# Writing out the matrix engine's loop over fifteen experts

## The reference, cut to what matters

```python
def ec_moe(h, router_w, w1, w3, w2):
    xt = h.reshape(B * T, D)
    cap = EC_FACTOR * (B * T) // N_EXPERTS          # 128 latent slots, 16 context slots
    aff = jax.nn.softmax((xt @ router_w).astype(jnp.float32), axis=-1)
    gate_vals, idx = lax.top_k(aff.T, cap)
    xe = xt[idx]
    hid = jax.nn.silu(jnp.einsum('ecd,edf->ecf', xe, w1)) * jnp.einsum('ecd,edf->ecf', xe, w3)
    ye = jnp.einsum('ecf,efd->ecd', hid, w2) * gate_vals[..., None]
    y = jnp.zeros_like(xt).at[idx.reshape(-1)].add(ye.reshape(-1, D).astype(xt.dtype))
```

## Time and profile before

| what | value |
|---|---|
| median of 3 runs | 1709.96 us (1709.06 to 1711.66) |
| profiled execution, its own time | 1710.03 us |
| its span, first to last instruction | 1708.3 us |
| PE busy, share of the span | 1633.5 us, 96% |
| DVE, ACT, POOL busy | 701.7, 395.3, 357.3 us |
| PE instructions: matmuls, weight loads | 11310, 11310 |
| mean granted TensorE clock | 0.983 |

### The profile page before, as it was taken

The page is one execution under the profiler, slowest core; times in us unless marked ns, Lnnn a source line. Parts: engine busy times, 40 slices in busy tenths (PEclk is TensorE's granted clock), DMA queues, the critical chain, the costliest instruction groups (busy, mean ns, idle before and its releaser), DMA issues. The chain is left out here.

```text
span 1708.3 us, 28611 instructions
## 1 busy us (share of the span) xinstructions
PE 1633.5 (96%) x11310; PEld 1420.4 (83%) x11310; DVE 701.7 (41%) x1778; ACT 395.3 (23%) x954; POOL 357.3 (21%) x427
## 2 busy tenths in 40 slices
PE   5999989999999899999989999999999999999997
PEld 4876866666568666788879999999999999999994
DVE  4001047785465888222363322333332233333225
ACT  5220113341212476211131111111111111111113
POOL 2000000015233643121113112222211222221111
PEclk9999989999899999999999999999999999999998
DMA  8411112133212676322179877878888888888862
GB/s 312 145 41 53 39 54 59 51 105 36 46 34 87 179 197 219 113 92 94 56 292 350 313 270 265 310 264 293 307 283 281 265 301 271 282 309 283 287 215 112
DMA packets 213442, 323.03 MB, mean 189 GB/s; under 512 B 29680, under 2 KB 102377, under 8 KB 213371
## 3 DMA queue, kind: packets, MB, share of 16 engines
q1 hardware_dynamic: 180731, 282.66, 46.6%
q0 software_dynamic: 8560, 16.39, 5.3%
q10 hardware_dynamic: 24080, 23.02, 4.9%
HBM read 293.85 MB, written 24.99 MB: 187 GB/s over the span
## 5 line engine op out<-in xcount | busy, mean ns | idle before, releaser
L1802 PE MATMUL psum<-arena 128*128 128x144 f32 x4096 | 507.6, 287 | 9.5 <-issue 7.4
L1802 PEld LDWEIGHTS psum<-arena 128*128 128x128 f32 x4096 | 504.3, 190 | 12.5 <-issue 12.5
L1812 PE MATMUL psum<-arena 128*128 128x144 f32 x2048 | 253.5, 286 | 0.0
L1812 PEld LDWEIGHTS psum<-arena 128*128 128x128 f32 x2048 | 251.8, 190 | 0.0
L1403 PE MATMUL psum<-arena 128*128 128x384 f32 x720 | 244.1, 494 | 0.0
L2454 DVE TENSOR_TENSOR arena<-gt,psum 128x144 f32<-128x144 f32 x128 | 39.0, 304 | 454.7 <-PE psum L1802 454.7
L852 POOL DMA_INDIRECT expert_list<-gt x128 | 126.2, 986 | 472.6 <-DVE gt L2440 426.2
L1403 PEld LDWEIGHTS psum<-arena 128*128 128x128 f32 x720 | 134.9, 192 | 91.5 <-issue 4.4
L1406 PE MATMUL psum<-arena 128*128 128x256 f32 (+2 forms) x864 | 165.5, 352 | 0.1
L1406 PEld LDWEIGHTS psum<-arena 128*128 128x128 f32 x864 | 145.7, 192 | 18.3 <-issue 1.7
L2324 DVE SCALAR_TENSOR_TENSOR arena<-arena,gt 128x1024 f32<-128x1024 f32 x128 | 159.0, 1280 | 0.6 <-DMA arena<-affinity_rows 0.6
(11 more groups left out here) (346 smaller groups left out, 1649.2 us busy)
## 6 DMA issues: line engine op xcount, KB each, us to landing
arena<-in_exp_w SPq DMA_DIRECT2D x96, 2048.0 KB, 9.0
arena<-in_ada_w SPq DMA_DIRECT2D x24, 1024.0 KB, 7.2
arena<-in_w_in SPq DMA_DIRECT2D x11, 1024.0 KB, 5.5
arena<-in_x_sample SPq DMA_DIRECT2D x16, 512.0 KB, 4.6
arena<-affinity_rows SPq DMA_DIRECT2D x16, 512.0 KB
arena<-m_decay_rows ACTq DMA_DIRECT2D x36, 128.0 KB, 3.3
arena<-decay_rows ACTq DMA_DIRECT2D x24, 192.0 KB, 3.6
out<-arena SPq DMA_DIRECT2D x9, 512.0 KB
```

Of the source, the lines that this page charges most:

```text
L1802: ins = mm(bank[:, 0:SLOTS], w[:, k, col], xeT[:, k, :], start=(k == 0), stop=(k == KD - 1))
L1812: ins = mm(bk[4 + db % 2][:, 0:SLOTS], wslot[4 + db // 4][:, k, (db % 4) * P:(db % 4) * P + P], hid[:, k, :], start=(k == 0), stop=(k == K ...
```

## The change

TensorE's loop over experts 0 to 14 is written out: the same calls in the same order, fifteen times, with `e` a number known when the program is built. The other engines keep their loops.

```diff
-            with pe.Fori(0, NE - 1) as e:
+            for e in range(NE - 1):
                 hidden(e)
                 pe.wait_ge(xgl_in, (e + 2) * 16)
                 pe.wait_ge(e_yeA, e + 1)
```

## The result

The changed kernel takes 1697.59 us (median of 5 runs, 1695.38 to 1701.87) against 1709.06 us (1708.33 to 1711.66) of the kernel before: ratio 0.9938, 95% interval 0.9927 to 0.995. Run again on another occasion (e2) it gave 0.9947, 0.9933 to 0.996. The forecast was 1702.5 us with a range from 1700.0 to 1705.8. By the medians the change won 11.5 us and 9.2 us; the forecast was 7.5 us, counted from the profiled execution's 1710.03 us, which lies 1.0 us above the median of 1709.06.

The account below looks back on a forecast made before the run. TensorE was taken to bound the expert stage, losing time only at the seams between rounds. 14 x (0.42 + 0.11) = 7.4 us plus 0.11 us at the exit gave 7.5 us: 1710.03 - 7.5 = 1702.5 us, range 1700.0 to 1705.8.

Parts of the forecast that it names:

- What bounds the kernel: In the expert stage TensorE is the path; the loop's whole cost to it sits at the seam between rounds.
- The seam's first term: At each of 14 jumps between rounds, PE idles 0.52 us against 0.10 at the loop's exit: 0.42 us won each.
- The seam's second term: At each seam, writing out also removes the compare and branch still left at the loop's exit: 0.11 us.
- The way in: Before round 0, up to 0.2 us of 2.06 us idle is the loop's, but the gather wait takes it back: 0.
- Instructions to fetch: In the expert stage, 45 more 16 KB instruction packets, fetched ahead of need: cost on the path 0.
- A: Rival: in the written-out expert code, 45 fetches each stop TensorE for 0.9 us, 40 us slower, 1742 us; chance 7%.
- B: Rival: the seam keeps most of its idle time, only the taken branch's extra 1.8 us is won, 1708.2 us; chance 6%.
- C: Rival: the seam vanishes altogether as the sequencer gets ahead, 9.9 us won, 1700.1 us; chance 10%.

Follow-up runs that it names:

- e2: The changed kernel, run again unchanged, against the kernel before; ratio 0.9947.
- e4: The changed kernel with the five waits before the next expert's hidden moved ahead of y_turned, for expert 0 ahead of all experts; ratio 0.9936.
- e5: The kernel before, loop kept, with the waits before the next expert's hidden moved ahead of y_turned, for expert 0 ahead of the loop; ratio 0.9959.
- e6: The changed kernel with a small two-round loop, waiting for a long fulfilled semaphore, put at 14 seams between experts; ratio 1.0019.
- e1: The kernel before, run again unchanged; ratio 0.9997.
- e3: The kernel before with TensorE's expert 0 alone written out and experts 1 to 14 left in the loop; ratio 0.9999.
- e7: The changed kernel with a small two-round loop once only, between the wait for expert 0's input and hidden(0); ratio 0.9954.
- e9: The kernel before, with its loop, plus four products nobody reads behind the first transposes of xg, where TensorE idles ahead of hidden(0); ratio 0.9997.
- e11: The same kernel as e4, run again beside e12; 1696.51 us, ratio 0.9931.
- e10: The kernel before with TensorE's expert 0 written out, then a loop of seven rounds of two experts each; 1726.8 us, ratio 1.0124.
- e8: The kernel before with TensorE's loop kept and the loops of ACT, DVE and POOL written out; ratio 0.9998.
- e12: The kernel of e4 with the loops of ACT, DVE and POOL written out as well; 1696.0 us, ratio 0.9933.

## Why the prediction was wrong

*What bounds the kernel*: right. The chain and its shares are the same after, and all that was won lies where TensorE was idle or slow.

*The seam's first term, jump against exit, 0.42 us*: right. The steps from matmul to matmul are 0.837 at a jump and 0.418 at the exit in both traces of before.

*The seam's second term, "what the exit still has of the loop", 0.11 us*: this failed. It measured 0.23 us (1.27 - 1.04 on PEld). I charged only the branch and kept the increment out of the sum. But the increment stands in the same row of sequencer steps, which begins at the last weight load of y_turned and goes on through branch and waits, about 0.1 us a step; written out, the first wait stands where the increment stood. So a seam is worth 0.65 us by PE's timeline instead of 0.53, and another 0.02 to 0.03 us since the 256 matmuls behind it take 31.60 us instead of 31.62; a round came out at 48.95 us instead of my 49.08. That the two waits go on costing about 0.1 us was right by e4, though no idle piece shows them. 14 x 0.12 + 0.12 + 14 x 0.025 = 2.1 us more than my term: 9.6 us by the rows, less 0.2 us for two seams of the profiled execution that took 0.28 and 0.35 us; why these two did is open, and e2 has none like them. e5 and e6 show the seam as a sum of the sequencer's steps, taken out and put in.

*The way in, counted at 0*: this failed too. I saw the 2.06 us of idle time and the 0.43 us that PE later waits for the gather, and concluded that anything won would be waited for, because the gather did not hang on TensorE's pace. Two things were otherwise. The first is the clock: `hidden(0)` ran 33.29 us against 31.62 in any other round. Both figures stood in my own rows, and the mean clock of 0.97 in the earlier trace rows; I didn't ask why they differ. With 0.35 us less idle time the lower clock did not come. The second is the gather: it did hang on TensorE's pace, by the 1.77 us that DVE waited for the first block in the middle of its ranking (0.55 us in e1, where the row to be ranked came later). So 1.8 us were won from the first transpose to the first matmul of `second(0)` (37.75 to 35.96 us), although the wait for the gather grew from 0.43 to 0.68. e3, e7 and e9 show the cause, and in their stretches 1.6 to 2.0 us. The size isn't fixed, though: in e6 and e11, with the full clock too, DVE got the row for its ranking 1.1 to 1.5 us later than in the changed kernel, the gather came 1.1 to 1.2 us later, and `second(0)` began only 37.1 and 37.0 us behind the first transpose. There half of the gain at the way in or more was waited for, as I had thought.

7.5 + 2.1 - 0.2 + 1.8 = 11.2 us, as measured between the stretches of the two profiled executions. That is 3.7 us of the 4.9 us between forecast and result; 1.0 us more is the base, 1710.03 instead of the median of 1709.06, and the last 0.2 us are scatter. Neither term would have left the range by itself: 1702.5 - 1.8 = 1700.7.

*Instructions to fetch, 0*: right. 44 to 45 packets in the expert stage, and not one idle piece of PE before L1802 or L1812 in the list of waits behind 920 us. The forecast count of 45 came out.

*Rivals.* A (exposed fetches) did not occur, but my price of 0.9 us has no measurement behind it: the only fetch that stopped TensorE, behind a taken branch in e10, cost 7.0 us, and no straight code shows one. B is out. C (the seam vanishes) is what happened in the idle list, and its 9.9 us was near the size of the seams, 9.4 to 9.6, but by luck: it is PEld's idle time, and no bound. e4's rounds are 0.78 us shorter than those with the loop, 11.0 us over 14, more than the 9.9 us that I had called the most.

*The range* ended at C alone. The unknown at the way in should have been bounded from both sides: at least 0, at most 33.29 - 31.62 + 0.2 = 1.9 us by its own rows and my own 0.2 us for the loop's share of the idle time. That would have put the low end at 1698.2, and with the scatter of -0.9 us, which I had left out of the low end, at 1697.3.

## What to carry to other kernels

Here the loop on the engine that bounds the kernel cost time only at the seam and at the way in, and at the seam it cost the sequencer's steps in a row: increment, branch, set-up and each wait with its computed number. Count them all from the last instruction that holds the sequencer, and move the waits that are long fulfilled ahead of it; that gave 0.40 of 0.65 us with the loop kept. A larger round was no safe middle way here: with two experts a round, two of six jumps cost more than ten times what a jump of the short loop did. Where the same group of instructions takes longer in one round than in the others, read the granted clock there before counting anything as hidden.

## What the runs showed of the hardware

- The clock behind a short idle time. In the five traces in which TensorE idled 2.06, 2.09, 1.90, 2.69 and 2.09 us ahead of `hidden(0)` (before, e1, e5, e7, e8) the lower level of 1.2 GHz follows, 0.5 to 1.3 us behind the first matmul and for 3.4 us; in the eight with 1.71 us (after, e2, e3, e4, e6, e10, e11, e12) and in e9, where the idle time was filled but for 0.33 us, it doesn't. At the 7.00 us of standstill in e10 it stood for 6.8 us, the last 3.6 of them behind the standstill.
- A taken compare and branch took 208 ns at most jumps and one not taken 76 ns; a wait 51 ns, with 0.1 us from one to the next.
- A round of 800 matmuls and weight loads was never fetched again in 695 us; one of 1600 was, at two jumps of six, with 7.0 us of standstill at each, 6.65 us of it in the branch at the one shown.
- In the kernel after, 44 instruction packets came between 929 and 1614 us beside a DMA share of 0.85, and PE was busy for 684.97 of these 685 us.
